# Two edits to a one-core decoder step: who asks for the sample's key and value pages, and what the projection's first work waits for

## The reference, cut to what matters

```
z      = rmsnorm(x) @ w_in                       # q, three k/v branches, gates, pool input
o_cmp  = attention over compressed blocks        # prompt, and sample over paged cache_cmp
o_sel  = attention over the top-k blocks         # sample: past blocks from paged cache_sel
o_win  = attention over the last 512 positions   # sample: cache_win
o      = g0*o_cmp + g1*o_sel + g2*o_win
h      = x + concat(o, pool_mix(u)) @ w_out
y      = h + peer(rmsnorm(h))                    # product-key retrieval of experts
```

## Time and profile before

| what | value |
|---|---|
| median of 3 runs | 1768.33 us |
| the profiled execution's own time | 1764.12 us |
| its span, first to last instruction | 1762.4 us |
| TensorE busy | 1682.8 us, 95% of the span |
| VectorE, ScalarE, GpSimd busy | 1369.0, 739.3, 457.6 us |
| mean granted TensorE clock | 0.975 |
| projection | up to about 163 us |
| attention | about 163 to 397 us |

### The profile page before, as it was taken

One profiled execution on the slowest core, in us unless ns is written; L12 is line 12 of the kernel. 1 busy time (PEld: TensorE's weight loads), 2 busy tenths in 40 slices (PEclk: granted clock), 3 DMA queues, 4 the chain that ended last, 5 costly groups with the idle time before them and its releaser, 6 DMA issues.

```text
span 1762.4 us, 29599 instructions
## 1 busy us (share of the span) xinstructions
PE 1682.8 (95%) x10384; PEld 1590.3 (90%) x10384; DVE 1369.0 (78%) x2809; ACT 739.3 (42%) x1392; POOL 457.6 (26%) x375
## 2 busy tenths in 40 slices
PE   7997988789999899999999999999999999999999
PEld 5876775559999899999999999999999899999999
DVE  3065335655578899999998998886898899999996
ACT  1023235434321433466665667863333333333333
POOL 0001100001100023333223225443344444444440
PEclk9898989789999999999999999999999999999999
DMA  9224412323322478988999889999899999999994
GB/s 305 66 62 154 128 44 67 88 64 96 108 70 64 138 273 293 328 294 316 313 323 318 311 286 371 365 367 385 309 382 381 367 403 395 400 397 391 396 393 165
DMA packets 196759, 457.31 MB, mean 259 GB/s; under 512 B 25842, under 2 KB 102898, under 8 KB 196146
## 3 DMA queue, kind: packets, MB, share of 16 engines
q1 hardware_dynamic: 123154, 252.34, 40.9%
q0 software_dynamic: 47440, 175.54, 26.8%
q10 hardware_dynamic: 26016, 27.53, 4.5%
HBM read 402.71 MB, written 56.05 MB: 260 GB/s over the span
## 4 chain that ended last, share of the span: by engine, by line
PE 60%; DVE 4%; DMA 1%; issue 1%; ACT 0%; SPq 0%; DVEq 0%; ACTq 0%; POOLq 0%
PE ps L1884 9%; PE ps L1881 9%; PE ps L1880 9%; PE ps L1908 9%; PE ps L1911 9%; PE ps L1914 9%; PE ps L1930 5%; DVE sb_w_lo L1713 1%; DMA sb_ring<-expert_v 1%; DVE sb_slot L1750 0%; DMA sb_expert_row<-expert_v,sb_row_expert 0%; DVE sb_rows_y L1843 0%; DVE sb_hot L1749 0%; ACT sb_w_hi L1617 0%; DVE sb_hot L1746 0%
## 5 line engine op out<-in xcount | busy, mean ns | idle before, releaser
L1617 ACT ACTIVATE sb_w_hi<-sb_ring 128x1024 fp32r<-128x1024 f32 x256 | 271.5, 1061 | 512.5 <-PE ps L1914 228.9
L1713 DVE TENSOR_TENSOR sb_w_lo<-sb_ring,sb_w_hi 128x1024 fp32r<-128x1024 f32 x256 | 313.5, 1225 | 65.2 <-ACT sb_w_hi L1617 57.8
L1880 PE MATMUL ps<-sb_x_hi,sb_w_hi 128*128 128x384 f32 x1024 | 351.5, 343 | 6.0 <-ACT sb_w_hi L1617 4.4
L1881 PE MATMUL ps<-sb_x_lo,sb_w_hi 128*128 128x384 f32 x1024 | 346.7, 339 | 0.0
L1884 PE MATMUL ps<-sb_x_hi,sb_w_lo 128*128 128x384 f32 x1024 | 201.9, 338 | 5.4 <-DVE sb_w_lo L1713 5.4
L1908 PE MATMUL ps<-sb_x_lo,sb_w_hi 128*128 128x384 f32 x1016 | 197.5, 336 | 4.8 <-ACT sb_x_lo L1626 4.8
L1880 PEld LDWEIGHTS ps<-sb_x_hi,sb_w_hi 128*128 128x128 f32 x1024 | 192.7, 188 | 6.6 <-ACT sb_w_hi L1617 6.6
L1914 PE MATMUL ps<-sb_x_lo,sb_w_hi 128*128 128x384 f32 x1016 | 197.1, 335 | 0.0
L1911 PE MATMUL ps<-sb_x_lo,sb_w_lo 128*128 128x384 f32 x1016 | 197.1, 335 | 0.0
L1881 PEld LDWEIGHTS ps<-sb_x_lo,sb_w_hi 128*128 128x128 f32 x1024 | 193.1, 189 | 0.0
L1884 PEld LDWEIGHTS ps<-sb_x_hi,sb_w_lo 128*128 128x128 f32 x1024 | 181.5, 187 | 7.7 <-DVE sb_w_lo L1713 7.7
(11 more groups left out here) (329 smaller groups left out, 2510.1 us busy)
## 6 DMA issues: line engine op xcount, KB each, us to landing
sb_ring<-expert_u SPq DMA_DIRECT2D x128, 512.0 KB
sb_ring<-expert_v SPq DMA_DIRECT2D x128, 512.0 KB
gates_dense<-sb_g_stage ACTq DMA_DIRECT2D x12, 2048.0 KB
hid_dense<-sb_hid SPq DMA_DIRECT2D x112, 192.0 KB
sb_scores<-hid_dense SPq DMA_DIRECT2D x112, 192.0 KB
sb_g_stage<-gates_dense SPq DMA_DIRECT2D x32, 384.0 KB
sb_g_stage<-gates_dense SPq DMA_DIRECT2D x48, 256.0 KB
sb_ring<-peer_wq SPq DMA_DIRECT2D x16, 512.0 KB
```

The costliest lines, as they stand in the source:

```text
L1617: nc.scalar.activation(whi[v % 2][:, :], ring(v)[:, :], ACT.Copy).then_inc(w_hi, 1)
L1713: nc.vector.tensor_tensor(wlo[v % 2][:, :], ring(v)[:, :], whi[v % 2][:, :], ALU.subtract).then_inc(w_lo, 1)
L1880: nc.tensor.matmul(out, hi[:, c * P:(c + 1) * P], g.x_hi[:, c], start=(c == 0), stop=False)
L1881: nc.tensor.matmul(out, hi[:, c * P:(c + 1) * P], g.x_lo[:, c], start=False, stop=False)
```

## The change

The load of `norm1` moves from ScalarE's list to the head of SP's, and raises `x_in[0]` in place of `first_in`. The first two chunks of x now wait for `x_in[0]` at 32, that is, for x and `norm1`; the other chunks wait for x alone. TensorE's and VectorE's first waits for `first_in` are gone, and the later waits for it are at 32 (`c_mean_d` and `c_eps`).

In attention, of each 32 pages SP asks for the first 14 and GpSimd for the other 18. GpSimd gets the same four waits that SP has. Its pages raise the semaphores of its `cache_cmp` pages, `g.page_pool`, and TensorE waits for both engines' shares.

```diff
         @block.sync
         def _(sp):
+            sp.dma_start(norm1[:, :], g.a["norm1"]).then_inc(x_in[0], 16)
             for k in range(4):
                 sp.dma_start(g.xT[:, 2 * k:2 * k + 2, :], g.a["xT"][:, 2 * k:2 * k + 2, :]).then_inc(x_in[k], 16)
...
         @block.tensor
         def _(pe):
-            pe.wait_ge(first_in, 48)
...
             last.then_inc(item_mm, 1)
-            pe.wait_ge(first_in, 48)
+            pe.wait_ge(first_in, 32)
             pe.wait_ge(sq_used, KC - 1)
...
-            act.dma_start(norm1[:, :], g.a["norm1"]).then_inc(first_in, 16)
             act.dma_start(g.ring[0][:, :], g.a["w_in"][TILES[0]]).then_inc(g.ring_in[0], 16)
...
             for k in range(KC):
-                act.wait_ge(x_in[k // 2], 16)
+                act.wait_ge(x_in[k // 2], 16 if k >= 2 else 32)
...
-            dve.wait_ge(first_in, 48)
             for k in range(KC):
-                dve.wait_ge(x_in[k // 2], 16)
+                dve.wait_ge(x_in[k // 2], 16 if k >= 2 else 32)
...
+        SP_ROWS, POOL_ROWS = range(0, 14), range(14, BPT * NPAGE)
+        def load_key_page(engine, bt, k):
+            n = page(engine, bt * BPT * NPAGE + k)
+            return engine.dma_start(ks[:, k // NPAGE, (k % NPAGE) * PAGE:(k % NPAGE + 1) * PAGE],
+                                    g.a["cache_sel_k"][bass.ds(n, 1)].rearrange("a p n -> p (a n)"))
...
-                for k in range(BPT * NPAGE):
-                    sp.dma_start(ks[:, k // NPAGE, (k % NPAGE) * PAGE:(k % NPAGE + 1) * PAGE],
-                                 g.a["cache_sel_k"][bass.ds(page(bt * BPT * NPAGE + k), 1)].rearrange("a p n -> p (a n)")).then_inc(k_in[bt], 16)
+                for k in SP_ROWS:
+                    load_key_page(sp, bt, k).then_inc(k_in[bt], 16)
...
         @block.gpsimd
+            for bt in range(2):
+                if bt:
+                    pool.wait_ge(s2_mm, 1)
+                else:
+                    pool.wait_ge(sub_mm, 4)
+                for k in POOL_ROWS:
+                    load_key_page(pool, bt, k).then_inc(g.page_pool[0], 16)
+                if bt:
+                    pool.wait_ge(so_mm, 1)
+                else:
+                    pool.wait_ge(sub_mm, 8)
+                for k in POOL_ROWS:
+                    load_value_page(pool, bt, k).then_inc(g.page_pool[1], 16)
...
-                pe.wait_ge(k_in[bt], 16 * BPT * (NPAGE + 1))
+                pe.wait_ge(k_in[bt], 16 * (BPT + len(SP_ROWS)))
+                pe.wait_ge(g.page_pool[0], 16 * (pool_pages(0) + (bt + 1) * len(POOL_ROWS)))
```

More of the change, by code:

```diff
@@ L394, in _ @@
                 nc.scalar.activation(sq[:, square_at(k)], g.xT[:, k], ACT.Square).then_inc(sq_ready, 1)
-            act.wait_ge(first_in, 48)
+            act.wait_ge(first_in, 32)
             act.wait_ge(sq_used, KC)
@@ L624, in attend, with page, load_value_page @@
                  [(1, ss[:, PAST:NS], ST), (2, sw[:, WIN:NW_], ST), (0, sc, NCMP_S)]
+        SP_ROWS, POOL_ROWS = range(0, 14), range(14, BPT * NPAGE)
+        pool_pages = lambda e: sum(32 * e <= k < 32 * e + 32 for x in POOL_PAGES for k in x)
+        def page(engine, n):
+            return engine.value_load(g.table[0:1, n:n + 1], min_val=0, max_val=NPHYS - 1)
+        def load_key_page(engine, bt, k):
+            n = page(engine, bt * BPT * NPAGE + k)
+            return engine.dma_start(ks[:, k // NPAGE, (k % NPAGE) * PAGE:(k % NPAGE + 1) * PAGE],
+                                    g.a["cache_sel_k"][bass.ds(n, 1)].rearrange("a p n -> p (a n)"))
+        def load_value_page(engine, bt, k):
+            n = page(engine, bt * BPT * NPAGE + k)
+            return engine.dma_start(vs[:, k // NPAGE, k % NPAGE], g.a["cache_sel_v"][bass.ds(n, 1)].rearrange("a p n -> p (a n)"))
         @block.sync
         def _(sp):
-            def page(n):
-                return sp.value_load(g.table[0:1, n:n + 1], min_val=0, max_val=NPHYS - 1)
             for e in range(2):
@@ L649, in _ @@
                     sp.dma_start(vw[:, b], g.a["cache_win_v"][bt * BPT + b]).then_inc(v_in[bt], 16)
-                for k in range(BPT * NPAGE):
-                    sp.dma_start(vs[:, k // NPAGE, k % NPAGE], g.a["cache_sel_v"][bass.ds(page(bt * BPT * NPAGE + k), 1)].rearrange("a p n -> p (a n)")).then_inc(v_in[bt], 16)
+                for k in SP_ROWS:
+                    load_value_page(sp, bt, k).then_inc(v_in[bt], 16)
         @block.gpsimd
@@ L722, in sub @@
                 pe.wait_ge(g.page_in[e], 16 * sum(32 * e <= k < 32 * e + 32 for x in SP_PAGES for k in x))
-                pe.wait_ge(g.page_pool[e], 16 * sum(32 * e <= k < 32 * e + 32 for x in POOL_PAGES for k in x))
+                pe.wait_ge(g.page_pool[e], 16 * pool_pages(e))
                 if m >= 2:
@@ L793, in row_values @@
             def row_values(bt):
-                pe.wait_ge(v_in[bt], 16 * BPT * (NPAGE + 1))
+                pe.wait_ge(v_in[bt], 16 * (BPT + len(SP_ROWS)))
+                pe.wait_ge(g.page_pool[1], 16 * (pool_pages(1) + (bt + 1) * len(POOL_ROWS)))
                 pe.wait_ge(s_t_act, 2 * bt + 2)
```

## The result

The changed kernel takes 1776.11 us (median of 17 executions), the kernel before 1771.24 us (17 executions beside them). The ratio of the executions is 1.0032 with a 95% interval of 1.0019 to 1.0046: 5.7 us slower, between 3.4 and 8.1 (the two medians alone differ by 4.9). The ratios leave out a few executions far above the rest: one of the kernel before at 2777 us, and two of the run pages_only at 2389 and 4579 us. So the changed kernel is slower, though by less than the 0.5% that the prediction set as its bound. The forecast was +4.4 us.

The account below looks back on a forecast made before the run. TensorE, busy 95% of the span, was taken as the bound. From 1768.3 us, +8.0 for the start and -3.6 for the pages gave +4.4, so 1772.7 us, range 1761 to 1779.

Parts of the forecast that it names:

- First matmul at 7.5 us, g = 4.8: Projection start: first matmul moves from 12.5 to 7.5 us; g, TensorE's lead when the second tile ends, is 4.8 us.
- out_win_past ahead of tile t=3: Projection: GpSimd issues the out_win_past copy at 25.9 us, before SP's load of tile t=3 at 28.2 to 28.7.
- The load lands behind the copy, at 43.5: Projection: the copy lands at 41.7 us, then tile t=3's own 0.5 MB takes 1.8 us, landing at 43.5.
- Fourth tile 5.8 us later, and 2.2 us of slow beginning: Projection: TensorE idles 10.6 us, goes on 5.8 us later than before, and pays the slow beginning again, 2.2 us.
- Part 1: The start's edits in the projection, in sum +8.0 us, bounds -6 to +13.7 us.
- The 3.6 us of the pages: Attention, second round: waits on selected keys (3.0 us) and values (0.7 us) go; taken as -3.6 us, bounds 0 to -5.5.
- The sum: Whole kernel: +8.0 for the start and -3.6 for the pages give +4.4 us, 1772.7 us.
- B: Rival: load of t=3 shares the engines fairly or comes first, no collision; -8.4 us, 1759.9 us; chance 0.14.
- D: Rival: the page edit gains nothing, its 3.6 us return as waits on VectorE's softmax chain; +8.0, 1776.3 us; chance 0.09.
- C: Rival: load of t=3 waits for both GpSimd copies, TensorE's wait ends after 46 us; +9.6, 1777.9 us; chance 0.15.
- the row that I had named to decide: TensorE's wait at line 278 on sb_ring, about 10 us from 33 us; none means B, ending after 46 means C.
- A: The forecast itself: the copy overtakes t=3's weights, attention's gain does not make it good; 1772.7 us, 1767 to 1778; chance 0.62.

Follow-up runs that it names:

- pages_only: The changed kernel with its projection edits taken back, so only the page split against the kernel before: 1768.49 us, ratio 0.9984 (0.9962 to 1.0007).
- copy_late: The changed kernel, with GpSimd's two copies waiting for the fourth tile in place of the second: 1761.05 us, ratio 0.9951 to the kernel before.
- before_copy_early: The kernel before, with GpSimd's two copies issued after the first tile in place of the second: 1780.9 us, ratio 1.0052.
- start_only: The kernel before with only the projection edits (norm1 on SP, first waits dropped), all pages still on SP: 1781.14 us, ratio 1.0058.
- before_copy_late: The kernel before, with GpSimd's two copies issued after the fourth tile in place of the second: 1771.92 us, ratio 0.9998.
- copy_pieces: The changed kernel with the 4064 KB copy walked in an order that can't be joined into long pieces: 1775.07 us, ratio 1.0035 to the kernel before.
- t3_early: The changed kernel, with SP asking for tile t=3's weights before the constants of later stages: 1759.41 us, ratio 0.9957 to the kernel before.

## Why the prediction was right in kind, and where it was off

**First matmul at 7.5 us, g = 4.8.** It came at 6.94 and g was 5.5 (copy at 25.21 against 30.74). Right, a little small. c_eps and c_mean_d cost nothing, as said.

**out_win_past ahead of tile t=3.** Forecast 25.9, and 28.2 to 28.7. Measured 25.21 and 30.66. The order is right. The load's issue is 2.0 us later than my latest figure, because I added only the 0.45 us of the new DMA to SP's list. SP reached `page_table` at 22.11 where it was 20.96 before, and one later issue took 1.68 us. The copy is not needed for this: in copy_late the load is issued at 30.49 too. That a copy can hold up SP's issues much more is shown by before_copy_early alone (4.72 and 4.09).

**The load lands behind the copy, at 43.5.** It came at 46.05. The copy's landing was forecast at 41.7 and measured at 40.8. The mis-sized term is the 1.8 us for "its own 0.5 MB at some 300 GB/s". It took 5.2 us. I had priced the load by its own bytes, as if it stood alone. Ahead of it in its queue were 0.3 MB in seven loads, which with its own bytes make 2.4 us at the measured 345 GB/s. And it is in only when the slowest of the 16 DMA engines has its share, 1.4 us behind the fifteenth (45.91 against 44.53), while the others already moved t=4 and t=5. How the remaining time divides was not settled.

**Fourth tile 5.8 us later, and 2.2 us of slow beginning.** Measured 8.4 and 3.2. Part 1 in sum was +8.0 in the forecast and 11.6 in the profile (46.05 - 37.7 + 3.2), and the same 11.6 stand at the first row scores.

**The 3.6 us of the pages.** 3.3 in the profile, by other terms. From the first row scores to the second it is 1.5 us less (58.5 before, 57.1 after): the wait of 3.12 has gone, but the work ahead of it took longer. The 16 matmuls take 1.6 us less, which I had as a bound only, and the values' 0.7 is gone; work elsewhere in the round took 0.5 longer. Yet the runs show that this term was no constant. All of start_only, before_copy_early and before_copy_late have another wait on SP's pages than the one I read. Measured from the first row scores to the end of attention they take 101.6, 101.7 and 105.4 us, where all kernels with the split take 100.6 to 100.8. So the split is worth 0.9 to 4.7 us, by where TensorE and SP's queue stand to each other.

**The sum.** The forecast was +4.4 us. The profiles give +11.6 - 3.3 = +8.3 at the end of attention. The ratio gives +5.7, 3.4 to 8.1, so a part of the profile's difference is this one execution's. The forecast's time is inside the interval; its two terms were 3.6 and 0.3 us too favourable by the profile.

**The rivals.** B (no collision, 1759.9) falls with the stall; its time is what the kernel takes once the order is mended (1759.41 and 1761.05). D (pages gain nothing, 1776.3) has the time measured but not the mechanism: the waits on keys and values are gone in the profile, though pages_only's interval reaches to zero. C said that the load waits for both copies and lands after 46. The second copy was issued at 25.9 and landed 16.7 us later, at 42.6, and TensorE's wait ended at 46.05. By the row that I had named to decide, C's mark is met by 0.05 us. But its price, +9.6 us, lies outside the interval, and the second copy's 0.18 MB is not what was waited for: from 40.8 us on GpSimd's queue had 8 packets and 0.02 MB, and SP's had 1.77 MB. The case lies between A and C, with SP's own queue behind the copy (small loads ahead of the tile, and one slow DMA engine), which I had in neither.

## What to carry to other kernels

Whoever makes one engine earlier should list what its progress triggers, and look at which requests of other queues the triggered transfer now precedes. A load that must come soon is worth moving ahead of those that need not. It is priced by all that stands before it in its queue, in packets as in bytes, and by the slowest DMA engine, not by its own bytes at the mean rate. Splitting the large transfer did not help it here. A wait between two engines that run a close race is not a constant of the kernel: look at it in several executions before its removal is entered as a gain.

## What the runs showed of the hardware

- A copy from memory to memory in pieces of 65,024 bytes leaves another queue almost nothing while it runs: 3.30 MB against 0.05 in 11 us. The turns are one for one by pieces (404 against 401 in copy_pieces).
- An engine's issue of a DMA can itself take several us in place of 0.43: 5.6 us at one of SP's behind its own loads, and 4.72 us at another that takes 0.43 in the kernel before, when only GpSimd's copy is moved ahead of it (before_copy_early).
- A load is in when the last of 16 DMA engines has its share. Here the shares of one 0.5 MB load landed over 3.5 us (42.40 to 45.91), with later loads already moving on other DMA engines.
- The 64 position-bias products of one column behind the fourth tile are some us longer or shorter from one profile to another. Over the eleven profiles they took 8.7 to 11.6 us; before 11.3 and in t3_early 8.8, in step with the granted clock (columns as above). First before, then t3_early:

```profile
44.90:56.20 11.30, 11.30 (x66) 11.27 (x64) 0.79 (x2) 0.00 (x0) 0.00 (x0) 0.61 0.58 150
```

```profile
38.90:47.70 8.80, 8.80 (x66) 8.79 (x64) 0.79 (x2) 0.00 (x0) 0.00 (x0) 0.80 0.92 242
```

No edit touches them, and what makes the clock fall at a given moment here was not settled.
